# A two-block transformer kernel on one core: input in four parts, norm gains over another queue, and the first unit's blocks between the input turns

## What is computed

```python
def _rmsnorm(x, g):
    x32 = x.astype(jnp.float32)
    y = x32 * lax.rsqrt(jnp.mean(x32 * x32, axis=-1, keepdims=True) + RMS_EPS)
    return (y * g.astype(jnp.float32)).astype(x.dtype)

def _swiglu(x, w_gate, w_up, w_down):
    return (jax.nn.silu(x @ w_gate) * (x @ w_up)) @ w_down

x = x + 0.5 * _swiglu(_rmsnorm(x, ffn1_norm[l]), ffn1_w_gate[l], ffn1_w_up[l], ffn1_w_down[l])
```

## Time and profile before

| | before |
|---|---|
| median of the runs | 3317.64 us |
| the profiled execution's own time | 3316.44 us |
| its span (first to last instruction) | 3314.6 us |
| TensorE busy | 3191.3 us, 96% of the span |
| VectorE busy | 1772.7 us, 53% |
| ScalarE busy | 1160.6 us, 35% |
| mean granted TensorE clock | 0.985 |
| DMA | 288 MB, mean 87 GB/s |

### The profile page before, as it was taken

One profiled execution on the slowest core, in us unless ns is written; L12 is line 12 of the kernel. 1 busy time (PEld: TensorE's weight loads), 2 busy tenths in 40 slices (PEclk: granted clock), 3 DMA queues, 4 the chain that ended last, 5 costly groups with the idle time before them and its releaser, 6 DMA issues.

```text
span 3314.6 us, 42521 instructions
## 1 busy us (share of the span) xinstructions
PE 3191.3 (96%) x14834; PEld 2559.8 (77%) x14834; DVE 1772.7 (53%) x2733; ACT 1160.6 (35%) x1895; POOL 543.8 (16%) x499
## 2 busy tenths in 40 slices
PE   8999998999999999988999989989999999999998
PEld 7788765788888888765888868667888886688887
DVE  4434477543445444585543443548647555576474
ACT  4323235322223222353322222534324334444242
POOL 0000335300020001254100030231000432310003
PEclk9999999999999999999999999999999999999998
DMA  4354421233333333211333333112333231123332
GB/s 122 99 141 142 123 64 33 77 97 94 98 98 95 101 89 104 78 51 40 94 103 92 101 97 89 39 51 70 109 87 103 68 98 39 52 70 99 94 97 78
DMA packets 541434, 287.99 MB, mean 87 GB/s; under 512 B 14419, under 2 KB 537398, under 8 KB 541328
## 3 DMA queue, kind: packets, MB, share of 16 engines
q1 hardware_dynamic: 535936, 273.32, 28.6%
q0 software_dynamic: 5392, 13.31, 1.4%
HBM read 284.30 MB, written 10.02 MB: 89 GB/s over the span
## 4 chain that ended last, share of the span: by engine, by line
PE 80%; DVE 10%; POOL 3%; issue 3%; ACT 2%; DMA 1%; DVEq 0%; ACTq 0%; POOLq 0%
PE bank L1791 65%; PE bank L1805 4%; PE bank L2042 2%; PE bank L1837 2%; PE bank L1900 1%; PE bank L2083 1%; PE bank L2106 1%; POOL probs L667 1%; DVE w_lo L1206 1%; ACT w_hi L755 1%; PE bank L1858 1%; DVE norm_t L1279 1%; PE bank L1878 1%; DVE score L1438 1%; POOL decay_q L726 0%
## 5 line engine op out<-in xcount | busy, mean ns | idle before, releaser
L755 ACT ACTIVATE w_hi<-w_raw 128x1024 fp32r<-128x1024 f32 (+2 forms) x477 | 533.1, 1119 | 1435.4 <-PE bank L1791 785.2
L1791 PE MATMUL bank<-h_hi,w_hi 128*128 128x512 f32 x2532 | 995.4, 393 | 9.7 <-DVE w_lo L1206 5.8
L1791 PE MATMUL bank<-h_hi,w_lo 128*128 128x512 f32 x2532 | 986.7, 390 | 0.0
L1791 PE MATMUL bank<-h_lo,w_hi 128*128 128x512 f32 x2520 | 981.8, 390 | 0.0
L1206 DVE TENSOR_TENSOR w_lo<-w_raw,w_hi 128x1024 fp32r<-128x1024 f32 (+1 forms) x445 | 617.3, 1388 | 471.3 <-ACT w_hi L755 471.1
L1791 PEld LDWEIGHTS bank<-h_hi,w_hi 128*128 128x128 f32 x2532 | 475.3, 188 | 121.2 <-issue 15.5
L1791 PEld LDWEIGHTS bank<-h_hi,w_lo 128*128 128x128 f32 x2532 | 475.1, 188 | 100.6
L1791 PEld LDWEIGHTS bank<-h_lo,w_hi 128*128 128x128 f32 x2520 | 473.3, 188 | 99.4 <-issue 1.9
L1791 PE MATMUL bank<-act_hi,w_hi 128*128 128x512 f32 x924 | 360.6, 390 | 0.0
L1791 PE MATMUL bank<-act_lo,w_hi 128*128 128x512 f32 x924 | 360.4, 390 | 0.0
L1791 PE MATMUL bank<-act_hi,w_lo 128*128 128x512 f32 x924 | 360.3, 390 | 0.0
(11 more groups left out here) (320 smaller groups left out, 3985.4 us busy)
## 6 DMA issues: line engine op xcount, KB each, us to landing
w_raw<-in_ffn_w_gate_dram SPq DMA_DIRECT2D x88, 512.0 KB, 3.8
w_raw<-in_ffn_w_up_dram SPq DMA_DIRECT2D x88, 512.0 KB, 3.8
w_raw<-in_ffn_w_down_dram SPq DMA_DIRECT2D x64, 704.0 KB, 4.5
w_raw<-in_ffn_w_in_dram SPq DMA_DIRECT2D x88, 512.0 KB, 3.8
w_raw<-in_ffn_w_out_dram SPq DMA_DIRECT2D x32, 704.0 KB, 4.5
w_raw<-in_w_in_dram SPq DMA_DIRECT2D x34, 512.0 KB, 3.8
w_raw<-in_a_w_qkv_dram SPq DMA_DIRECT2D x24, 512.0 KB, 3.7
w_raw<-in_w_out_dram SPq DMA_DIRECT2D x16, 512.0 KB, 3.6
```

The costliest lines, as they stand in the source:

```text
L755: nc.scalar.activation(w_hi[c % 2][:, 0:nk, 0:cols], raw[c % 2][:, 0:nk, 0:cols], ACT.Copy).then_inc(hi_ready, 1)
L1791: mm = nc.tensor.matmul(result(c)[0:cols, :], w[b][:, k, 0:cols], x[k], start=(k == 0 and n == 0), stop=(k == nk - 1 and n == 2))
```

## The change

The input comes in four DMAs of 256 channels each (`X_PARTS`), each with its own semaphore, and the weights of unit 0 are issued between the first and the second part. The 11 DMAs of the gains move from SP's queue to ScalarE's, ahead of everything else there. TensorE turns the gains first, then blocks 0 to 5 of the input, then does blocks 0 to 3 of unit 0, turns blocks 6 and 7, and does blocks 4 to 7 of unit 0. ScalarE and VectorE make `h_hi` and `h_lo` of two blocks behind each pair of turned blocks. The spread product moves from behind unit 1 to behind unit 2. Two of the four sums of squares move ahead of the high part of unit 2.

```diff
-            sp.dma_start(xtok[:, :, :], A["x"][0].rearrange("(t p) d -> p t d", p=P)).then_inc(x_in, 16)
-            load(0, kview(A["ffn1_w_gate"], 0)[:, :, 0:P])
+            for a in range(X_PARTS):
+                cols = slice(D // X_PARTS * a, D // X_PARTS * (a + 1))
+                sp.dma_start(xtok[:, :, cols], A["x"][0][:, cols].rearrange("(t p) d -> p t d", p=P)).then_inc(x_in[a], 16)
+                if a == 0:
+                    load(0, kview(A["ffn1_w_gate"], 0)[:, :, 0:P])
             load(1, kview(A["ffn1_w_up"], 0)[:, :, 0:P])
-            for n, g in enumerate(GAINS):
...
-                sp.dma_start(gain_rows[gain_at[g, 0]:gain_at[g, 0] + rows, :], src).then_inc(gains_in, 16)
...
@@ scalar
+            for n, g in enumerate(GAINS):
...
+                act.dma_start(gain_rows[gain_at[g, 0]:gain_at[g, 0] + rows, :], src).then_inc(gains_in, 16)
             for k in range(0, KT, 2):
+                if k == 0:
+                    act.wait_ge(gains_turned, 1)
+                    nc.scalar.activation(gains[:, :], bank[5][:, 0:P], ACT.Copy).then_inc(rows_out, 1)
                 act.wait_ge(x_turned, k + 1)
                 nc.scalar.activation(xres[:, k, :], bank[0][:, :], ACT.Copy).then_inc(bank_free[0], 1)
-                if k == 2:
+                if k == 0:
+                    act.wait_ge(rows_out, 1)
+                h_high(stages[0], k)
+                h_high(stages[0], k + 1)
+                if k == 0:
                     hi(0)
-            act.wait_ge(gains_turned, 1)
-            nc.scalar.activation(gains[:, :], bank[5][:, 0:P], ACT.Copy).then_inc(rows_out, 1)
-            act.wait_ge(rows_out, 1)
-            for k in range(KT):
-                h_high(stages[0], k)
             hi(1)
...
                 if name == stages[0]:
+                    token_squares(range(2))
+                hi(c + 2)
+                if name == stages[0]:
                     token_root()
-                hi(c + 2)
@@ vector
             for k in range(1, KT, 2):
                 dve.wait_ge(x_turned, k + 1)
                 nc.vector.tensor_copy(xres[:, k, :], bank[1][:, :]).then_inc(bank_free[1], 1)
-                if k == 3:
+                if k == 1:
+                    dve.wait_ge(rows_out, 1)
+                h_low(stages[0], k - 1)
+                h_low(stages[0], k)
+                if k == 1:
                     lo(0)
-            for k in range(KT):
-                h_low(stages[0], k)
             lo(1)
...
-                if name == stages[0]:
-                    token_diag()
                 if name != "final":
                     lo(c + 2)
+                    if name == stages[0]:
+                        token_diag()
@@ tensor
                     elif name == stages[0]:
-                        gemm(c, H_HI, H_LO, h_ready, count)
+                        for k in range(4, KT):
+                            if k % 2 == 0:
+                                turn_input(k)
+                                turn_input(k + 1)
+                            gemm_blocks(c, range(2 * k - 8, 2 * k - 6), H_HI, H_LO, h_ready, count)
                         gemm(c + 1, H_HI, H_LO, h_ready, count)
+                        gemm(c + 2, H_HI, H_LO, h_ready, count)
                         pe.wait_ge(tok_spread, 1)
                         nc.tensor.matmul(STATB[:, :], ones[:, :], rms[:, :],
                                          start=True, stop=True).then_inc(sum_ready, 1)
...
+            def turn_input(k):
+
+                pe.wait_ge(x_in[k // (KT // X_PARTS)], 16)
                 if k >= 2:
                     pe.wait_ge(bank_free[k % 2], k // 2)
                 for t in range(NT):
                     mm = nc.tensor.transpose(bank[k % 2][:, P * t:P * (t + 1)], xtok[:, t, P * k:P * (k + 1)], ident[:, :])
                 mm.then_inc(x_turned, 1)
+
+            pe.wait_ge(consts, 1)
             pe.wait_ge(gains_in, 16 * len(GAINS))
             nc.tensor.transpose(bank[5][:, 0:P], gain_rows[:, :], ident[:, :]).then_inc(gains_turned, 1)
+            for k in range(4):
+                turn_input(k)
...
                             first_units(name, c, h0)
-                            gemm(c + 2, H_HI, H_LO, h_ready, h0)
+                            if name != stages[0]:
+                                gemm(c + 2, H_HI, H_LO, h_ready, h0)
```

More of the change, by code:

```diff
@@ L34 @@
 MIX_Q = 10
+X_PARTS = 4
 KI_COLS = D_IN - W_IN_COLS[KI] * P
@@ L345, in program @@
         bank_free = [sem("bank_free0"), sem("bank_free1")]
-        consts, x_in, x_turned = sem("consts"), sem("x_in"), sem("x_turned")
+        consts, x_turned = sem("consts"), sem("x_turned")
+        x_in = [sem(f"x_in{a}") for a in range(X_PARTS)]
         gains_in, rows_in, gains_turned, rows_turned, rows_out = (
@@ L526, in columns @@
                         load(c + s, w[:, :, DS(P * s + 2 * P * j, P)], j)
-            sp.dma_start(xtok[:, :, :], A["x"][0].rearrange("(t p) d -> p t d", p=P)).then_inc(x_in, 16)
-            load(0, kview(A["ffn1_w_gate"], 0)[:, :, 0:P])
-            load(1, kview(A["ffn1_w_up"], 0)[:, :, 0:P])
-            for n, g in enumerate(GAINS):
-                rows = GAIN_ROWS.get(g, 1) * KT
-                src = A[g].rearrange("l (k p) -> (l k) p", p=P) if len(A[g].shape) == 2 else \
-                    A[g].rearrange("(k p) -> k p", p=P)
-                sp.dma_start(gain_rows[gain_at[g, 0]:gain_at[g, 0] + rows, :], src).then_inc(gains_in, 16)
+            for a in range(X_PARTS):
[3 more added lines that the diff above has]
+                    load(0, kview(A["ffn1_w_gate"], 0)[:, :, 0:P])
+            load(1, kview(A["ffn1_w_up"], 0)[:, :, 0:P])
             sp.dma_start(few_rows[0:DEPTH, :], A["kv_norm_c"]).then_inc(rows_in, 16)
@@ L1036, in head_slots, with token_squares @@
                 sub_high(7)
+            for n, g in enumerate(GAINS):
+                rows = GAIN_ROWS.get(g, 1) * KT
+                src = A[g].rearrange("l (k p) -> (l k) p", p=P) if len(A[g].shape) == 2 else \
+                    A[g].rearrange("(k p) -> k p", p=P)
+                act.dma_start(gain_rows[gain_at[g, 0]:gain_at[g, 0] + rows, :], src).then_inc(gains_in, 16)
             for k in range(0, KT, 2):
+                if k == 0:
+                    act.wait_ge(gains_turned, 1)
+                    nc.scalar.activation(gains[:, :], bank[5][:, 0:P], ACT.Copy).then_inc(rows_out, 1)
                 act.wait_ge(x_turned, k + 1)
                 nc.scalar.activation(xres[:, k, :], bank[0][:, :], ACT.Copy).then_inc(bank_free[0], 1)
-                if k == 2:
-                    hi(0)
-            act.wait_ge(gains_turned, 1)
-            nc.scalar.activation(gains[:, :], bank[5][:, 0:P], ACT.Copy).then_inc(rows_out, 1)
-            act.wait_ge(rows_out, 1)
-            for k in range(KT):
-                h_high(stages[0], k)
-            hi(1)
+                if k == 0:
[3 more added lines that the diff above has]
+                if k == 0:
+                    hi(0)
+            hi(1)
+            def token_squares(tiles):
+                for landed in x_in:
+                    act.wait_ge(landed, 16)
+                for t in tiles:
+                    ins = nc.scalar.activation(tok_sq[:, t, :], xtok[:, t, :], ACT.Square, accum_out=tok_sum[:, t:t + 1])
+                return ins
             def token_root():
[L1053 to L1056, removed]
+                token_squares(range(2, NT)).then_inc(tok_step, 1)
                 nc.scalar.activation(spare[:, :], eps_c[:, :], ACT.Sqrt)
@@ L1801, in gemm_blocks @@
                         pe.wait_ge(lo_ready, c + 1)
-                        pe.wait_ge(bank_free[c % 2], XT_USES + c // 2)
+                        if c not in FIRST:
+                            pe.wait_ge(bank_free[c % 2], XT_USES + c // 2)
                     pe.wait_ge(ready, count + k + 1)
                     for n, (w, x) in enumerate(((w_hi, x_hi), (w_hi, x_lo), (w_lo, x_hi))):
-                        mm = nc.tensor.matmul(bank[c % 2][:, :], w[c % 2][:, k, :], x[k],
+                        mm = nc.tensor.matmul(result(c)[:, :], w[c % 2][:, k, :], x[k],
                                               start=(k == 0 and n == 0), stop=(k == KT - 1 and n == 2))
@@ L2141, in pair_slots @@
                 gemm_blocks(q0 + NP + 1, range(7, KT), *of_heads)
-            pe.wait_ge(consts, 1)
-            pe.wait_ge(x_in, 16)
-            for k in range(KT):
+            def turn_input(k):
+                pe.wait_ge(x_in[k // (KT // X_PARTS)], 16)
                 if k >= 2:
```

## The result

| | before | changed |
|---|---|---|
| median of 10 runs each | 3318.33 us (3314.91 to 3320.66) | 3325.24 us (3322.14 to 3331.53) |
| ratio | | 1.0019, 95% interval 1.0011 to 1.0028 |
| profiled execution: own time, span | 3316.44, 3314.6 us | 3327.54, 3325.7 us |

The change makes the kernel slower by 0.19%, about 6 us, right at the bound of 0.2% that I had set for telling a difference. The forecast was 3323.0 us, with 3316.5 to 3328.5 as range.

A forecast was written before the change was run, and what follows sets the result against it. TensorE, busy 96% of the span, was taken to bound the kernel. Opening 0.05, spread 3.8 and clock 1.5 summed to +5.3 us on 3316.44, plus 1.2 for the median: 3323.0 us, range 3316.5 to 3328.5.

The forecast's parts named there:

- What bounds, and where to look: Whole kernel: TensorE bound, busy 96% of the span; the start of unit 4, 41.8 us before, decides the change's effect.
- The spread product: Before unit 4: its 10.1 us chain has only 6.3 us of cover, so TensorE waits 3.8 us for `w_lo`.
- The clock behind the wait: Behind unit 4's wait: the granted clock falls to half, costing +1.5 us, bounds 0 and 3.
- The gains: Start of the opening: gains issued on ScalarE's queue by 4.9 us land at 7.5, bounds 6.5 and 11.
- Rival 2: TensorE's first instruction: ScalarE's issues held behind big transfers, gains land at 10 to 11, 3326 us; chance 0.17.
- The opening: Up to unit 1: unit 0 starts at 15.0, but unit 1 at 24.6 against 24.55 before, so nothing is won.
- The clock in the opening: Blocks 0 to 3 of unit 0: clock falls again to 1.2 GHz for part; bounds 1.2 us better or worse.
- The sum: Whole kernel: opening 0.05, spread 3.8 and clock 1.5 give +5.3 us.
- Rivals 1, 3 and 4: 1: unit 4's chain has cover, 3316.4 us, 0.08; 3: opening loads don't overlap, 3324, 0.05; 4: clock stays up, 3320, 0.15.

The follow-up runs named there:

- after_again: The changed kernel, unaltered, measured again on another chip against the kernel before: 3325.00 against 3317.44 us, ratio 1.0023.
- a_spread_back: The changed kernel with the spread product back between units 1 and 2: 3320.75 us against 3319.92 for the kernel before, ratio 1.0005.
- b_before_spread_late: The kernel before with only the spread product moved behind unit 2: 3321.84 us against 3319.92 for the kernel before, ratio 1.0013.
- c_first_gain_apart: The changed kernel, its start waiting only for the first gain DMA, other gains turned later: 3321.22 us against 3319.92 for the kernel before, ratio 1.0004.
- d_gains_unloaded: The changed kernel, with SP holding all big transfers behind input part 0 until all gains have landed: one run, 3328.05 us.
- f_all: e_split_spread plus unit 1's weights split behind block 5, blocks 6 and 7 turned behind two blocks of unit 0: 3312.60 against 3317.44 us before, ratio 0.9986.
- e_split_spread: c_first_gain_apart with the spread product inside unit 2, behind 2 of its 8 blocks: 3316.08 us against 3317.44 for the kernel before, ratio 0.9993.
- h_before_gains_act: The kernel before with only the 11 gain DMAs moved to ScalarE's queue: 3319.85 us against 3318.97 for the kernel before, ratio 1.0003.

## Why the prediction was right, and where it wasn't

**What bounds, and where to look: right.** TensorE's own work and the start of unit 4 decided. The 7.2 us at unit 6 are about what the runs show for the whole kernel (6.3 by the ratio, 6.9 by the medians).

**The spread product: right, and shown.** 3.8 us forecast, 3.65 measured, in the changed kernel, in after_again, and in the kernel before with this one move alone. The chain from the spread product to unit 4's `w_lo` was forecast at 10.1 us and is 10.15 (37.40 to 47.55). The table load in it took 1.28 us again. The 2.7 us of the Trainium skill (ScalarE: Activation LUTs, "What ACT_TABLE_LOAD costs") are for the whole switch: about 1.28 for the load, and about 1.38 for a drain. The load agrees with the trace. The drain doesn't show in it: the load starts within 0.02 us of the end of `rstd` (38.46 + 0.60, then 39.07), and Silu starts 0.02 us behind the load. So the row of the trace was the right price. The 1.5 us that I put on a wait for the diagonal behind unit 1 measured 0.94, in a_spread_back.

**The clock behind the wait: right for this case, too narrow as a rule.** +1.5 forecast; from start to start units 4 and 5 took 12.33 us and not 10.88, which is 1.45. Behind the same wait of 3.65 us it was 2.9 in b_before_spread_late, 3.0 in c_first_gain_apart and 1.7 in after_again. So the point was met by luck of this trace, and the upper bound of 3 was the better part of that estimate.

**The gains: the failed step.** The text said "a small DMA lands 2.2 us after issue ... and with the big transfers beside them I take 7.5". The issues ended at 5.4, near the 4.9 expected, but the last landed at 10.26. The 2.2 us came from 32 DMAs far behind the opening (2709 to 2739 us), while the queues moved 89 GB/s on the mean; they took 1.5 to 3.7 us, and the row has only their median. d_gains_unloaded shows 1.78 with nothing big in flight and the changed kernel 5.30 for the loaded case. Rival 2 had the time (10 to 11) and the wrong mechanism: its issues were to be held, and none was. I also read the sharing rule of the Trainium skill (DMA: Bandwidth & Descriptors, "Queues, rings and completion order") as speaking against a delay. Taking turns packet by packet doesn't keep a small transfer ahead; it spreads its packets over the time of the big ones, and the trace agrees with that reading: 169 of 256 packets were still to come behind the last issue. The row that would have warned me was in my hands: in the kernel before, 3 MB are on the way at 290 to 409 GB/s until about 11 us, and with the gains beside them I added only 0.4 us.

**The opening: wins nothing, but by another sum.** Forecast unit 1 at 24.6 (+0.05), measured 26.4 (+1.8). The gains landed 2.8 us later than forecast (10.3 for 7.5), and unit 0 started 2.7 later (17.7 for 15.0); 1.0 us was made up because the clock was at full speed from about 19.7 on, so that blocks 6 and 7 were turned in 0.8 us and not in 1.8. That unit 1 waits last for its own `w_lo` was right (0.38 us), and f_all confirms it.

**The clock in the opening: right for the kernel before, wrong for the changed one.** In the kernel before, the clock rose at 13.8 us, and was down from 17.2 to 20.6, a fall that begins in TensorE's idle time of 2.0 us; unit 0 lost some 1.5 us by it (6.91 us from start to start against 5.44), near the 1.2 of my sum. For the changed kernel I forecast a second such fall. None came in its first profile: the clock hadn't risen yet when unit 0 began, and rose at 19.7 us (see below). Blocks 0 to 3 took 3.8 us where I had 3.9, so the size was met by luck and not by the cause I gave. In after_again the clock did fall there, as forecast.

**The sum.** Forecast 5.3 us; at unit 6 it is 7.2: 1.8 from the opening where 0.05 stood, 3.9 from unit 1 to unit 4 (the wait of 3.65 and two slow starts) where 3.8 stood, and 1.5 from the clock as forecast. The runs say 6 to 8 (the first comparison and after_again). That puts the truth between the forecast and rival 2: the time was met within its range, with the opening too cheap by 1.8 us. Rivals 1, 3 and 4 did not come: the chain had no cover, the first two parts of the input landed as reckoned (4.8 and 8.1 in c_first_gain_apart, forecast 4.6 and 7.9), and the clock fell.

## What to carry to other kernels

When a step is moved one unit later to spare a wait, count the chain that starts behind it: here 0.94 us of waiting for a diagonal (a_spread_back) was traded for 3.65 us of waiting for what the diagonal feeds, plus the clock. Put such a step inside a unit, at the block where its input is ready, and let the start wait only for the rows it uses: with these two (e_split_spread) unit 6 starts 3.3 us ahead of the kernel before instead of 7.2 behind it. With the reordering of f_all on top the runs are clear of noise, about 4.6 us faster than the kernel before instead of 6 slower, though the traces don't put that last step's gain in the opening. And price a small DMA by what is in flight beside it, not by its own size.

## What the runs showed of the hardware

**A small DMA beside big ones.** The last of 11 gain DMAs (8 KB) took 1.78 us from issue to landing with nothing big in flight (d_gains_unloaded), 5.30 us with three quarters of the input and the weight tiles, up to 2.5 MB, in flight (changed kernel); the 2 MB input took 7.6 us without the gains beside it and 8.3 us with them (h_before_gains_act).

**The granted clock ahead of its first record.** In the changed kernel the row of the stretch from 17.7 us says 1.00:

```profile
17.70:19.50 1.80, 1.80 (x6) 1.50 (x5) 1.80 (x3) 1.58 (x3) 0.00 (x0) 1.00 0.84 223
```

But its matmuls last 0.63 us (the one at 18.73 in the timeline of the changed kernel), as at half clock in the earlier trace rows, where 6 of them took 2.70 us; at full clock they last 0.39. Eight transposes took 1.97 us in c_first_gain_apart's opening, and these take half in the changed kernel's later turns:

```profile
21.51 1.04 PE L2173 MATMUL bank<-ident,xtok 128*128 128x128 f32 x8
```

So TensorE starts at 1.2 GHz in every trace here, and the 1.00 shown ahead of its rise is no measurement. In the changed kernel it rose at 19.7 us. In the kernel before it rose at 13.8: the turn at 14.88 takes 0.66 us for the 4 transposes that take 1.09 at half clock (the changed kernel's at 15.61).

```profile
14.88 0.66 PE L2152 MATMUL bank<-ident,xtok 128*128 128x128 f32 x4 [0.34 <-DVE xres L1632]
```

The 0.50 of the earlier trace rows at 17.6 us is therefore a real fall, behind an idle time of 2.0 us. h_before_gains_act has the same idle time of 2.0 us ahead of unit 0, and no fall: its matmuls stand 0.23 us apart from the start. Durations of equal instructions tell the clock; the row doesn't until it has changed once.

**The scatter is mostly the clock.** Nearly the same opening gave profiled spans of 3325.7 and 3320.2 us. Behind unit 6 TensorE worked 80.2 us at half clock in the first and 60.0 in the second; half of that difference is 10.1 us, of which 3.8 went into longer idle times, and 6.3 are what the rest of the kernel was shorter by. The runs of the kernel before lie between 3311.3 and 3324.0, 0.4% apart. Which of the later short waits are followed by a fall of the clock differs from trace to trace, and the fall behind unit 4's wait cost 1.5 to 3.0 us.
